# Sample attention of a decoder step: the third sequence's rope keys are turned earlier, and the last output but one is turned ahead of two score turnings

## The chip, the cores and the metric

The kernel runs on one core of a Trainium2 chip. The metric is the device time of one execution in microseconds (us); lower is better. Five engines work side by side: TensorE (PE, with its weight loads shown as PEld), VectorE (DVE), ScalarE (ACT), GpSimd (POOL) and SyncE (SP), which issues the loads of weights and cache pages. Each works through its own instructions in order, and they meet at semaphores.

## The reference, cut to what matters

The program is one inference step of a two-layer decoder. It serves one prompt of 512 tokens and 8 sample sequences of 8 new tokens, each with 2048 cached positions in 16 pages of 128. The change touches only the attention of the samples, which works on the latent cache:

```
past = cache_latent[l][page_table].reshape(8, 2048, 288)      # 256 latent | 32 rope
keys = concatenate([past, latent], axis=1)
q_lat = einsum('bqhn,chn->bqhc', q_nope, w_uk)
s = einsum('bqhd,bkd->bhqk', [q_lat | q_rope], keys) * ATTN_SCALE     # masked
p = softmax(s)
o_lat = einsum('bhqk,bkd->bqhd', p, keys[..., :256])
o = einsum('bqhc,chv->bqhv', o_lat, w_uv)
```

Ahead of it in a layer come the projections and the prompt's own attention, behind it the output projection, a convolved feed-forward part and, after both layers, a norm.

## The kernel before, in words

One program per engine is written out by hand, and the order in it is the order of execution. The order of TensorE in the sample attention, per layer, is `all_scores(0)`, then for b = 1 to 7 `all_scores(b)` and `all_values(b-1)`, then `all_values(7)` and `turn_output(7)`. So the values of a sequence come one place behind its scores, and between the scores of sequences 0 and 1 there are no values.

A sequence's 2048 keys lie in its pages with positions on the partitions. To be multiplied they are turned over (multiplied with the identity into PSUM, eight banks of 128 x 512) and copied to SBUF:

- `turn_rope(b)` (PE L1950) turns the 32 rope columns of all 16 pages into one bank (bank 6 for b > 0). It needs all 16 pages of the sequence: it waits for the four semaphores `pages_in[b % 3][g]`. DVE's `rope_keys(b)` (L1348) copies the bank to `ropeT[b % 2]`.
- `turn_keys(b, g)` (PE L1520, a helper's line that all turnings share) turns the latent part of four pages, for g = 0 to 3, into banks 4 and 5. ACT (`keys`, L805) and DVE (`keys`, L1352) copy one bank each.
- For b = 1 two more turnings follow `turn_keys(1, 0)`: those of the new tokens' latents `ckv`, into bank 7.
- `rope_scores(b)` (PE L1994) starts the scores in banks 0 to 3. For b > 0 it waits for `s_exp(b)`, the exponentials of sequence b-1 (ACT L820 and L822, released by a drain at L824), which read those banks. `scores(b, g)` (L2000) adds the latent part, and DVE takes the maxima (L1362 to L1387), which the exponentials wait for.
- `all_values(b)` turns the exponentials `sc` in five pieces (`turn_scores(b, g)`, L1520), copied to `pT` by ACT (g = 0 and 2, L829) and DVE (g = 1, 3 and 4, L1392 to L1400), and multiplies them with the pages (`values`, L2047, then L2076) into bank 7. DVE scales the result into `olat` (L1402), `turn_output(b)` turns it (L1520), and ACT copies it to `olatT` (`latent_output`, L811).

For the last sequence, `all_values(7)` holds `turn_output(6)`, behind `turn_scores(7, 0)`, `(7, 1)` and `(7, 2)`. The first values wait for `latent_output(6)`, since both use bank 7. ACT's order there is the copies of g = 0 and g = 2 and then `latent_output(6)`.

The pages have three buffers. SyncE issues one DMA of 144 KB per page, in order: the 16 pages of sequence 0, the 16 of sequence 1 (after the prompt's keys are assembled), and the 16 of sequence 2 (`keys_of(2)`, behind a wait for the last pair of prompt heads, `pv`). Then come the load of `wuv` (L491) and, from the third on, the pages of sequence b, each behind the values of sequence b-3 (`spv`, L478).

Of the kernel before, what the change touches and what calls it, by code (L numbers as in the profile page):

```python
# [31 lines left out]
TP, NB, NS = 512, 8, 8  # L32
# [51 lines left out]
def build(nc, A, O):  # L84
# [215 lines left out]
    kt_p, kt_d, kt_a = signal("kt_p", 5 * NB), signal("kt_d", 5 * NB), signal("kt_a", 4 * NB)  # L300
    newk_T, newk_ev = signal("newk_T", 1), signal("newk_ev", 1)
    s_p, s_new, new_ev = signal("s_p", 4 * NB), signal("s_new", NB), signal("new_ev", NB)
# [31 lines left out]
    def keys_bank(b, g):  # L334

        return 1 if b == 0 and g == 0 else 4

    def rope_bank(b):

# [8 lines left out]
    with nc.Block() as block:  # L348
# [208 lines left out]
        def _(act):  # L557
# [23 lines left out]
            for f in range(KD):  # L581
                act.wait_ge(start_T.sem, f + 1)
                b = 2 * (f % 2)
# [43 lines left out]
            for l in range(DEPTH):  # L627
# [173 lines left out]
                turned_probs(NH - 1)  # L801

                def keys(b, g):
                    act.wait_ge(kt_p.sem, kt_p.at(l, 5 * b + g + 2))
                    nc.scalar.activation(keysT[g % 2][:, 0, :], PS[:, keys_bank(b, g), :], ACT.Copy).then_inc(kt_a.sem, 1)  # L805

                def latent_output(b):

                    act.wait_ge(so_T.sem, so_T.at(l, b + 1))
                    for c in range(KC):  # L810
                        last = nc.scalar.activation(olatT[:, c, :, b, :], PS[:, 7, 256 + 128 * c:384 + 128 * c].rearrange("p (h s) -> p h s", h=NH), ACT.Copy)  # L811
                    last.then_inc(so_a.sem, 1)
# [10 lines left out]
                                         bias=softm[:, o + 6:o + 7], scale=SCALE, accum_out=softm[:, o + 8:o + 9])  # L823
                    nc.scalar.drain().then_inc(s_exp.sem, 1)  # L824

                def turned_scores(b):
                    for g in (0, 2):
                        act.wait_ge(spt_p.sem, spt_p.at(l, 5 * b + g + 1))
                        nc.scalar.activation(pT[:, 4 * g:4 * g + 4, :].rearrange("p a b -> p (a b)"), PS[:, 4 + g, :], ACT.Copy).then_inc(spt_a.sem, 1)  # L829

                for b in range(NB):
# [11 lines left out]
                    if b >= 1:  # L843
                        turned_scores(b - 1)
                    exponentials(b)
                turned_scores(NB - 1)
                latent_output(NB - 2)
                hi(l, U_OUT, 0, 0)
                hi(l, U_OUT + 1, 0, 1)

# [166 lines left out]
        def _(dve):  # L1017
# [105 lines left out]
            for l in range(DEPTH):  # L1123
# [220 lines left out]
                        last.then_inc(qrs_ready.sem, 1)  # L1344

                def rope_keys(b):
                    dve.wait_ge(kt_p.sem, kt_p.at(l, 5 * b + 1))
                    v.tensor_copy(ropeT[b % 2][:], PS[:, rope_bank(b), :]).then_inc(kt_d.sem, 1)  # L1348

                def keys(b, g):  # L1350
                    dve.wait_ge(kt_p.sem, kt_p.at(l, 5 * b + g + 2))
                    v.tensor_copy(keysT[g % 2][:, 1, :], PS[:, keys_bank(b, g) + 1, :]).then_inc(kt_d.sem, 1)  # L1352

                rope_keys(0)
# [15 lines left out]

                def scores(b):
                    o = 16 + 16 * (b % 2)
                    if b > 0:
                        rope_keys(b)
                        keys(b, 0)
                    keys(b, 1)
                    maximum(b, 0)
                    keys(b, 2)
                    maximum(b, 1)
                    keys(b, 3)  # L1380
                    maximum(b, 2)
                    new_scores(b)
                    maximum(b, 3)
                    v.drain()
                    v.tensor_reduce(softm[:, o + 5:o + 6], softm[:, o:o + 5], AX.X, ALU.max)
                    v.drain()
                    v.tensor_scalar(softm[:, o + 6:o + 7], softm[:, o + 5:o + 6], -SCALE, None, ALU.mult).then_inc(s_max.sem, 1)  # L1387
# [126 lines left out]
        def _(pe):  # L1514
# [170 lines left out]
            for l in range(DEPTH):  # L1685
# [152 lines left out]
                for i, (kind, m) in enumerate(GATE_UNITS):  # L1838
                    u = U_GATE + i
                    use(l, u)  # L1840
                    if kind == "pool":
                        if m == 0:
                            pe.wait_ge(last_ev.sem, last_ev.at(l, 1))
                        for t in range(4 * m, 4 * m + 4):
                            g = t // 2
# [93 lines left out]

                def turn_rope(b):  # L1940

                    if b >= 2:
                        pe.wait_ge(spt_a.sem, spt_a.at(l, 2 * (b - 1)))
                    if b >= 1:
                        pe.wait_ge(new_ev.sem, new_ev.at(l, b))
                    for g in range(4):
                        pe.wait_ge(pages_in[b % 3][g].sem, pages_in[b % 3][g].at(l, 16 * 4 * (b // 3 + 1)))
                    for t in range(4):
                        for g in range(4):
                            r = mm(PS[32 * g:32 * g + 32, rope_bank(b), 128 * t:128 * t + 128], pages[b % 3][:, 4 * g + t, KVL:LAT], ident[:], start=True, stop=True)  # L1950
                    r.then_inc(kt_p.sem, 1)

                def turn_keys(b, g):

                    if b >= 2 and g == 0:
                        pe.wait_ge(spt_a.sem, spt_a.at(l, 2 * (b - 1)))
                        pe.wait_ge(spt_d.sem, spt_d.at(l, 3 * (b - 1)))
                    if b > 0 or g > 0:
                        pe.wait_ge(kt_a.sem, kt_a.at(l, 4 * b + g))
                        pe.wait_ge(kt_d.sem, kt_d.at(l, 5 * b + g + (g > 0)))  # L1960
                    for c in range(KC):
                        for j in range(4):
                            r = turn(PS[:, keys_bank(b, g) + c, 128 * j:128 * j + 128], pages[b % 3][:, 4 * g + j, 128 * c:128 * c + 128], 128)
                    r.then_inc(kt_p.sem, 1)
# [19 lines left out]

                def rope_scores(b):

                    pe.wait_ge(kt_d.sem, kt_d.at(l, 5 * b + 1))
                    if b > 0:
                        pe.wait_ge(s_exp.sem, s_exp.at(l, b))
                    else:  # L1990
                        pe.wait_ge(kt_a.sem, kt_a.at(l, 1))
                        pe.wait_ge(kt_d.sem, kt_d.at(l, 2))
                    for g in range(4):
                        mm(PS[:, g, :], query(qrs[32 * g:32 * g + 32], b), ropeT[b % 2][32 * g:32 * g + 32, :], start=True, stop=False)  # L1994

                def scores(b, g):
                    pe.wait_ge(kt_a.sem, kt_a.at(l, 4 * b + g + 1))
                    pe.wait_ge(kt_d.sem, kt_d.at(l, 5 * b + g + 2))
                    for c in range(KC):
                        r = mm(PS[:, g, :], query(qlat[:, c], b), keysT[g % 2][:, c, :], start=False, stop=c == KC - 1)  # L2000
                    r.then_inc(s_p.sem, 1)
# [10 lines left out]
                    r.then_inc(so_T.sem, 1)  # L2012

                def all_scores(b):
                    if b > 0:
                        turn_rope(b)
                        turn_keys(b, 0)
                    if b == 1:
                        pe.wait_ge(o_done.sem, o_done.at(l, NH // 2))
                        for c in range(KC):  # L2020
                            r = turn(PS[0:TS, 7, 128 * c:128 * c + 128], ckv[:, c, TP:T], 128)
                        r.then_inc(newk_T.sem, 1)
                    rope_scores(b)
                    turn_keys(b, 1)
                    scores(b, 0)
                    if b >= 2:
                        turn_output(b - 2)
                    turn_keys(b, 2)
                    scores(b, 1)
                    turn_keys(b, 3)  # L2030
                    scores(b, 2)
                    new_scores(b)
                    scores(b, 3)
# [15 lines left out]
                def all_values(b):  # L2049
                    pe.wait_ge(s_exp.sem, s_exp.at(l, b + 1))  # L2050
                    if b + 1 < NB:
                        pe.wait_ge(new_ev.sem, new_ev.at(l, b + 2))
                    else:
                        pe.wait_ge(spt_a.sem, spt_a.at(l, 2 * b))
                        pe.wait_ge(spt_d.sem, spt_d.at(l, 3 * b))
                    turn_scores(b, 0)
                    turn_scores(b, 1)
                    turn_scores(b, 2)
                    if b == NB - 1:
                        turn_output(b - 1)  # L2060
                    if b == 0:
                        pe.wait_ge(newk_ev.sem, newk_ev.at(l, 1))
                    else:
                        pe.wait_ge(so_a.sem, so_a.at(l, b))
                    pe.wait_ge(spt_a.sem, spt_a.at(l, 2 * b + 1))
                    values(b, 0)
                    turn_scores(b, 3)
                    pe.wait_ge(spt_d.sem, spt_d.at(l, 3 * b + 1))
                    turn_scores(b, 4)
                    values(b, 1)  # L2070
                    pe.wait_ge(spt_a.sem, spt_a.at(l, 2 * b + 2))
                    values(b, 2)
                    pe.wait_ge(spt_d.sem, spt_d.at(l, 3 * b + 2))
                    values(b, 3)
                    pe.wait_ge(spt_d.sem, spt_d.at(l, 3 * b + 3))
                    mm(PS[:, 7, 0:KVL], pT[0:TS, NPG, :], newk[:], start=False, stop=True).then_inc(spv.sem, 1)  # L2076
# [150 lines left out]
```

## Time and profile before

| | us |
|---|---|
| Median of 3 runs | 2269.22 (2268.37 to 2270.55) |
| Profiled execution, its own time | 2268.8 |
| Its span, first to last instruction | 2267.0 |
| PE busy | 2217.9 (98%) |
| DVE / ACT / POOL busy | 1170.7 / 877.6 / 656.8 |
| Mean granted TensorE clock | 0.995 of full |

The span starts with the first instruction, and all times in the trace count from there. The profiled execution's own time is 1.8 us longer than its span. The first layer's sample attention runs from about 465 to 655 us, the second's from about 1577 to 1767 us. A busy share alone does not tell whether an engine sets the time; the wait of each instruction on PE does, and the rows below are of that kind.

### The profile page before, as it was taken

The numbers are of one execution on the slowest core, as the hardware profiler recorded it, in microseconds if no ns is written. First come the engines' busy times: TensorE is split into PE (matmuls) and PEld (weight loads), VectorE is DVE, ScalarE is ACT, GpSimd is POOL, SyncE is SP. The second block draws the span as 40 slices with busy tenths as digits, with TensorE's granted clock in tenths as the row PEclk, the third lists the DMA queues.
The fourth block names the chain that finished last, engine by engine and source line by source line (L and its number), as shares of the span: only waits on it lengthen the run. The fifth ranks groups of instructions, "written<-read, shape, count | busy, mean of one in ns | idle before, by whom it ended". The sixth has DMA issues, their size and how long they took to land.

```text
span 2267.0 us, 42639 instructions
## 1 busy us (share of the span) xinstructions
PE 2217.9 (98%) x16207; PEld 1988.3 (88%) x16207; DVE 1170.7 (52%) x1831; ACT 877.6 (39%) x1879; POOL 656.8 (29%) x316
## 2 busy tenths in 40 slices
PE   6999999999999999999999999999999999999998
PEld 5899997667789999999988999966677999999998
DVE  4443753844346666651153717457443476666433
ACT  4223225832233555541132332367222345555322
POOL 0223434400022333333322334332000323333332
PEclk9999999999999999999999999999999999999999
DMA  8554332033342222235545433212332422222322
GB/s 300 166 146 98 87 84 65 14 109 108 88 127 88 83 83 83 83 105 166 175 124 176 83 98 84 76 43 61 96 107 55 157 71 83 78 80 83 87 84 84
DMA packets 338278, 230.69 MB, mean 102 GB/s; under 512 B 62732, under 2 KB 321605, under 8 KB 338140
## 3 DMA queue, kind: packets, MB, share of 16 engines
q1 hardware_dynamic: 336594, 226.37, 34.8%
q10 hardware_dynamic: 1546, 2.43, 0.3%
q8 instruction: 92, 1.51, 0.3%
q14 instruction: 46, 0.38, 0.1%
HBM read 223.15 MB, written 5.60 MB: 101 GB/s over the span
## 4 chain that ended last, share of the span: by engine, by line
PE 93%; ACT 3%; DVE 2%; DMA 1%; issue 0%; DVEq 0%; SPq 0%; ACTq 0%
PE PS L1552 62%; PE PS L1520 6%; PE PS L2000 5%; PE PS L2047 5%; PE PS L1833 2%; PE PS L1596 2%; PE PS L1648 2%; PE PS L1936 2%; ACT prob L777 1%; PE PS L1569 1%; PE PS L1889 1%; PE PS L1912 1%; PE PS L1994 1%; PE PS L1950 1%; PE PS L2076 0%
## 5 line engine op out<-in xcount | busy, mean ns | idle before, releaser
L977 POOL TENSOR_TENSOR wlo<-raw,whi 128x1024 fp32r<-128x1024 f32 (+1 forms) x248 | 586.6, 2366 | 1503.0 <-ACT whi L563 1503.0
L563 ACT ACTIVATE whi<-raw 128x1024 fp32r<-128x1024 f32 (+1 forms) x252 | 258.6, 1026 | 927.1 <-PE PS L1552 852.2
L1552 PE MATMUL PS<-h_hi,whi 128*128 128x288 f32 x2496 | 538.6, 297 | 1.2 <-issue 1.0
L1552 PE MATMUL PS<-h_lo,whi 128*128 128x288 f32 x2496 | 535.4, 296 | 0.0
L1552 PE MATMUL PS<-h_hi,wlo 128*128 128x288 f32 x2496 | 535.0, 296 | 0.0
L1552 PEld LDWEIGHTS PS<-h_hi,whi 128*128 128x128 f32 x2496 | 402.4, 189 | 9.6 <-issue 8.8
L1552 PEld LDWEIGHTS PS<-h_lo,whi 128*128 128x128 f32 x2496 | 403.3, 188 | 0.0
L1552 PEld LDWEIGHTS PS<-h_hi,wlo 128*128 128x128 f32 x2496 | 403.2, 188 | 0.0
L1454 DVE TENSOR_SCALAR conv<-zext,convp 128x592 f32<-128x592 f32 x88 | 153.7, 1747 | 135.4 <-ACTq L896 135.0
L1552 PE MATMUL PS<-act_hi,whi 128*128 128x288 f32 x704 | 153.0, 299 | 0.0
L1552 PE MATMUL PS<-act_lo,whi 128*128 128x288 f32 x704 | 151.0, 296 | 0.0
L1552 PE MATMUL PS<-act_hi,wlo 128*128 128x288 f32 x704 | 150.9, 296 | 0.0
L2000 PE MATMUL PS<-keysT,qlat 128*128 128x512 f32 x256 | 122.1, 600 | 0.0
L2047 PE MATMUL PS<-pages,pT 128*128 128x256 f32 x512 | 117.0, 382 | 1.6 <-ACT olatT L811 1.6
L1552 PEld LDWEIGHTS PS<-act_hi,whi 128*128 128x128 f32 x704 | 113.2, 189 | 5.5 <-issue 5.3
L1552 PEld LDWEIGHTS PS<-act_lo,whi 128*128 128x128 f32 x704 | 113.8, 189 | 0.0
L1552 PEld LDWEIGHTS PS<-act_hi,wlo 128*128 128x128 f32 x704 | 113.6, 189 | 0.0
L2047 PEld LDWEIGHTS PS<-pages,pT 128*128 128x128 f32 x512 | 95.0, 190 | 15.0 <-ACT olatT L811 2.1
L1117 DVE SCALAR_TENSOR_TENSOR x<-PS,mod,x 128x288 f32<-128x288 f32 x32 | 16.6, 517 | 173.1 <-PE PS L1552 163.8
L805 ACT ACTIVATE keysT<-PS 128x512 f32<-128x512 f32 x64 | 38.3, 598 | 138.9 <-PE PS L1520 138.7
L1046 DVE TENSOR_TENSOR sumsq<-sumsq,tmp 128x576 f32<-128x576 f32 x30 | 49.1, 1637 | 80.3 <-ACT tmp L938 64.9
L1912 PE MATMUL PS<-k,q 96*128 96x128 f32 (+3 forms) x256 | 79.8, 454 | 6.1 <-ACT prob L777 6.1
(288 smaller groups left out, 3327.9 us busy)
## 6 DMA issues: line engine op xcount, KB each, us to landing
raw<-w_up SPq DMA_DIRECT2D x88, 512.0 KB, 3.8
pages<-cache_latent SPq DMA_DIRECT2D x256, 144.0 KB, 2.1
raw<-w_in SPq DMA_DIRECT2D x64, 512.0 KB, 4.0
ada_ring<-w_ada SPq DMA_DIRECT2D x41, 512.0 KB, 4.9
raw<-w_down SPq DMA_DIRECT2D x32, 512.0 KB, 3.9
ada_next<-w_ada SPq DMA_DIRECT2D x17, 512.0 KB, 4.1
ada_first<-w_ada SPq DMA_DIRECT2D x16, 512.0 KB, 10.4
raw<-w_out SPq DMA_DIRECT2D x16, 512.0 KB, 4.2
```

The costliest lines, as they stand in the source:

```text
L563: nc.scalar.activation(whi[:, slot, 0:width(u)], raw[:, slot, 0:width(u)], ACT.Copy).then_inc(hi_ready.sem, 1)
L977: nc.gpsimd.tensor_tensor(wlo[:, slot, 0:n], raw[:, slot, 0:n], whi[:, slot, 0:n].bitcast(F32), ALU.subtract).then_inc(lo_ready.sem, 1)
L1046: v.tensor_tensor(sumsq[:], sumsq[:], tmp[:, s, :], ALU.add).then_inc(sq_used.sem, 1)
L1454: v.tensor_scalar(c, zext[:, s, 2:ZE], convp[:, 1, bass.ds(f, 1)], convp[:, 1, bass.ds(f + 2 * KF, 1)], ALU.mult, ALU.add)
L1520: return nc.tensor.transpose(out, src, ident[0:k, 0:k])
L1552: r = mm(PS[0:m, 2 * (j % pairs) + half, 0:HT], w, o[:, k0 + k, half * HT:half * HT + HT], start=(first and k == 0 and part is whi and o i ...
L1596: r = mm(PS[:, 2 * s + half, 0:HT], part[:, s, 128 * k:128 * k + 128], o[:, k, half * HT:half * HT + HT], start=k == 0 and part is whi and ...
L1648: o = mm(PS[32 * j:32 * j + 32, 4 + r % 2, 0:256], cond[:, k, :], src[:, 256 * j:256 * j + 256], start=k == 0, stop=k == KD - 1)
L1833: r = mm(PS[:, bank, 0:c1 - c0], part[:, s, w0 + step * k:w0 + step * k + 128], o[:, k, c0:c1], start=(k == 0 and part is whi and o is xh) ...
L1912: mm(PS[:, qb, 0:128 * (qb + 1)], q96[:, s, 128 * qb:128 * qb + 128], k96[:, s, 0:128 * (qb + 1)], start=True, stop=True).then_inc(qk.sem, 1)
L2000: r = mm(PS[:, g, :], query(qlat[:, c], b), keysT[g % 2][:, c, :], start=False, stop=c == KC - 1)
L2047: mm(PS[:, 7, 0:KVL], pT[:, j, :], pages[b % 3][:, j, 0:KVL], start=j == 0, stop=False)
```

## The change

It has two parts, made in the programs of TensorE, VectorE and ScalarE; SyncE's and GpSimd's are as before. First, `turn_rope(2)` goes from the head of `all_scores(2)` into `all_scores(1)`, behind `turn_keys(1, 0)` and ahead of the two turnings of `ckv` and of `rope_scores(1)`. It waits for the copy of sequence 1's rope keys out of bank 6 and, as before, for all pages of sequence 2. DVE's `rope_keys(2)` goes to the matching place, between `keys(1, 0)` and `keys(1, 1)`, and the counts on the two semaphores are renumbered. Second, `turn_output(6)` comes right behind `turn_scores(7, 0)`, and ACT's `latent_output(6)` between the copies of g = 0 and g = 2.

```diff
+    def turned_rope(b):
+        return 8 if b == 2 else 5 * b + 1
+    def turned_keys(b, g):
+        return 5 * b + g + (3 if b == 1 and g > 0 else 2)
...                                                   ScalarE
-                turned_scores(NB - 1)
+                turned_scores(NB - 1, (0,))
                 latent_output(NB - 2)
+                turned_scores(NB - 1, (2,))
...                                                   VectorE, scores(b)
+                    if b == 1 or b > 2:
+                        rope_keys(b)
                     if b > 0:
-                        rope_keys(b)
                         keys(b, 0)
+                    if b == 1:
+                        rope_keys(2)
                     keys(b, 1)
...                                                   TensorE, turn_rope(b)
-                    if b >= 2:
+                    if b == 2:
+                        pe.wait_ge(kt_d.sem, kt_d.at(l, turned_rope(1)))
+                    elif b >= 1:
+                        pe.wait_ge(new_ev.sem, new_ev.at(l, b))
+                    if b > 2:
                         pe.wait_ge(spt_a.sem, spt_a.at(l, 2 * (b - 1)))
-                    if b >= 1:
-                        pe.wait_ge(new_ev.sem, new_ev.at(l, b))
                     for g in range(4):
                         pe.wait_ge(pages_in[b % 3][g].sem, pages_in[b % 3][g].at(l, 16 * 4 * (b // 3 + 1)))
...                                                   TensorE, all_scores(b)
+                    if b == 1 or b > 2:
+                        turn_rope(b)
                     if b > 0:
-                        turn_rope(b)
                         turn_keys(b, 0)
                     if b == 1:
+                        turn_rope(2)
                         pe.wait_ge(o_done.sem, o_done.at(l, NH // 2))
...                                                   TensorE, all_values(b)
                     turn_scores(b, 0)
+                    if b == NB - 1:
+                        turn_output(b - 1)
                     turn_scores(b, 1)
                     turn_scores(b, 2)
-                    if b == NB - 1:
-                        turn_output(b - 1)
```

## Rows read from the trace of the kernel before

**Rows 1.** The page: the span, and busy time (share of the span) xinstructions

```profile
span 2267.0 us, 42639 instructions
PE 2217.9 (98%) x16207; PEld 1988.3 (88%) x16207; DVE 1170.7 (52%) x1831; ACT 877.6 (39%) x1879; POOL 656.8 (29%) x316
```

**Rows 2.** Waits of PE, whole span: us in total, times, longest us

```profile
PE PS L1994 <- ACTq L824: 3.0, 2, 1.5
```

**Rows 3.** Timeline, sequence 1, layer 1: start, duration, engine, ... [idle before <-releaser]

```profile
476.97 1.08 PE L1950 MATMUL PS<-ident,pages 128*32 128x128 f32 x32
477.98 1.09 PE L1520 MATMUL PS<-ident,pages 128*128 128x128 f32 x8
...
478.74 0.68 DVE L1348 COPY ropeT<-PS 128x512 f32<-128x512 f32 x1
...
478.91 0.38 PE L1520 MATMUL PS<-ident,ckv 128*64 128x128 f32 x2
...
480.46 0.19 ACT L822 ACTIVATION_READ_ACCUMULATOR sc<-newsc,softm 128x1 f32 x1
...
480.81 1.14 PE L1994 MATMUL PS<-ropeT,qrs 32*128 32x512 f32 x8 [1.52 <-ACTq L824]
...
483.02 0.69 DVE L1352 COPY keysT<-PS 128x512 f32<-128x512 f32 x1 [3.00 <-PE PS L1520]
```

**Rows 4.** Timeline, SyncE: first and last page of sequence 2, layers 1 and 2

```profile
467.58 1.42 SPq L479 DMA_DIRECT2D pages<-cache_latent  x2
...
483.92 0.33 SPq L479 DMA_DIRECT2D pages<-cache_latent  x1
...
1595.31 0.33 SPq L479 DMA_DIRECT2D pages<-cache_latent  x1
```

**Rows 5.** Line L479, the issues at 483.92 and at 1595.31: us to landing

```profile
DMA to landing us min/median/max: 2.2/2.2/2.2
...
DMA to landing us min/median/max: 2.4/2.4/2.4
```

**Rows 6.** Timeline, layer 2, the rope scores of sequence 1

```profile
1592.56 1.14 PE L1994 MATMUL PS<-ropeT,qrs 32*128 32x512 f32 x8 [1.52 <-ACTq L824]
```

**Rows 7.** Timeline, layer 1, sequence 2: exponentials before it, first keys, rope scores

```profile
498.57 0.19 ACT L822 ACTIVATION_READ_ACCUMULATOR sc<-newsc,softm 128x1 f32 x1
...
503.02 1.09 PE L1520 MATMUL PS<-ident,pages 128*128 128x128 f32 x8
503.16 0.69 DVE L1348 COPY ropeT<-PS 128x512 f32<-128x512 f32 x1 [0.56 <-PE PS L1950]
...
504.05 1.14 PE L1994 MATMUL PS<-ropeT,qrs 32*128 32x512 f32 x8
```

**Rows 8.** Timeline, layer 1, the start of the last sequence's values

```profile
642.72 1.53 PE L1520 MATMUL PS<-ident,sc 128*128 128x128 f32 x12
...
642.83 0.48 DVE L1402 TENSOR_SCALAR olat<-PS,softm 128x256 f32<-128x256 f32 x1 [5.04 <-PE PS L2076]
...
644.28 0.60 ACT L829 ACTIVATE pT<-PS 128x512 f32<-128x512 f32 x1 [0.28 <-PE PS L1520]
...
644.77 0.44 ACT L811 ACTIVATE olatT<-PS 128x128 f32<-128x128 f32 x2
...
645.27 1.99 PE L2047 MATMUL PS<-pages,pT 128*128 128x256 f32 x8 [0.80 <-ACT olatT L811]
```

**Rows 9.** Timeline, PE, the first matmul after its longest wait past 20 us

```profile
45.43 0.58 PE L1596 MATMUL PS<-h_hi,whi 128*128 128x288 f32 x1 [4.07 <-DVE h_lo L1089]
```

**Rows 10.** Windows: length, busy (x) of PE, PEld, DVE, ACT, POOL, PEclk, DMA, GB/s

```profile
43.00:44.00 1.00, 0.00 (x0) 0.00 (x0) 0.93 (x3) 0.71 (x1) 0.00 (x0) 0.95 1.08 285
...
50.00:51.00 1.00, 1.00 (x7) 1.00 (x6) 1.00 (x2) 0.61 (x1) 0.00 (x0) 0.64 1.04 396
...
46.00:50.00 4.00, 4.00 (x19) 4.00 (x18) 4.00 (x7) 2.27 (x4) 0.00 (x0) 0.50 1.01 342
...
52.00:56.00 4.00, 4.00 (x33) 4.00 (x32) 3.22 (x5) 1.45 (x2) 0.00 (x0) 1.00 0.12 49
```

More of the change, by code:

```diff
@@ L803, in keys @@
                 def keys(b, g):
-                    act.wait_ge(kt_p.sem, kt_p.at(l, 5 * b + g + 2))
+                    act.wait_ge(kt_p.sem, kt_p.at(l, turned_keys(b, g)))
                     nc.scalar.activation(keysT[g % 2][:, 0, :], PS[:, keys_bank(b, g), :], ACT.Copy).then_inc(kt_a.sem, 1)
@@ L824, in exponentials, with turned_scores @@
                     nc.scalar.drain().then_inc(s_exp.sem, 1)
-                def turned_scores(b):
-                    for g in (0, 2):
+                def turned_scores(b, groups=(0, 2)):
+                    for g in groups:
                         act.wait_ge(spt_p.sem, spt_p.at(l, 5 * b + g + 1))
@@ L1346, in rope_keys @@
                 def rope_keys(b):
-                    dve.wait_ge(kt_p.sem, kt_p.at(l, 5 * b + 1))
+                    dve.wait_ge(kt_p.sem, kt_p.at(l, turned_rope(b)))
                     v.tensor_copy(ropeT[b % 2][:], PS[:, rope_bank(b), :]).then_inc(kt_d.sem, 1)
                 def keys(b, g):
-                    dve.wait_ge(kt_p.sem, kt_p.at(l, 5 * b + g + 2))
+                    dve.wait_ge(kt_p.sem, kt_p.at(l, turned_keys(b, g)))
                     v.tensor_copy(keysT[g % 2][:, 1, :], PS[:, keys_bank(b, g) + 1, :]).then_inc(kt_d.sem, 1)
@@ L1959, in turn_keys @@
                         pe.wait_ge(kt_a.sem, kt_a.at(l, 4 * b + g))
-                        pe.wait_ge(kt_d.sem, kt_d.at(l, 5 * b + g + (g > 0)))
+                        pe.wait_ge(kt_d.sem, kt_d.at(l, turned_keys(b, g - 1) if g > 0 else turned_keys(b - 1, 3)))
                     for c in range(KC):
@@ L1985, in rope_scores @@
                 def rope_scores(b):
-                    pe.wait_ge(kt_d.sem, kt_d.at(l, 5 * b + 1))
+                    pe.wait_ge(kt_d.sem, kt_d.at(l, turned_rope(b)))
                     if b > 0:
@@ L1997, in scores @@
                     pe.wait_ge(kt_a.sem, kt_a.at(l, 4 * b + g + 1))
-                    pe.wait_ge(kt_d.sem, kt_d.at(l, 5 * b + g + 2))
+                    pe.wait_ge(kt_d.sem, kt_d.at(l, turned_keys(b, g)))
                     for c in range(KC):
```

## The prediction

> **What bounds the kernel now.** I read the page first: PE is busy for 98% of the span [rows 1], so the time is PE's own work plus its few waits, and a change counts by what it does to PE's order of work. Then the list of PE's waits: the wait ahead of `rope_scores(1)` for the exponentials of sequence 0 stands there with 3.0 us, 1.5 us in each of the two layers [rows 2]. The timeline around it shows what PE, DVE and ACT do there [rows 3]. Last I read the queue that nobody shows among PE's waits, SyncE's page loads [rows 4], since the moved turning reads pages.
>
> **Part 1, the wait that is to be filled.** PE starts the two `ckv` turnings at 478.91; they end at 478.91 + 0.38 = 479.29, and `rope_scores(1)` starts at 480.81, behind the last exponential (480.46 + 0.19 = 480.65) [rows 3]. The turning itself takes 477.98 - 476.97 = 1.01 us of PE, start to next start [rows 3]. By the engines alone it would fit: bank 6 is copied out at 478.74 + 0.68 = 479.42, so `turn_rope(2)` could start at 479.5, end its issue at 480.5, and with 0.3 us for the `ckv` turnings (from their 0.38, less the overlap of the last one's end) `rope_scores(1)` would start at 480.8, where it starts today. DVE's added copy (0.69 us) lies in the 3.00 us that DVE idles ahead of 483.02 [rows 3]; without that cover it would delay `keys(1, 1)` by the same 0.69.
>
> **Part 1, the pages.** The moved turning keeps its wait for all 16 pages of sequence 2. SyncE issues them one by one: the first at 467.58, the last at 483.92, which is (483.92 - 467.58) / 15 = 1.09 us apart [rows 4], and no part of the change makes this earlier. They follow the pages of sequence 1 without a gap, so it is SyncE's pace and not the `pv` wait that places them. The last page lands 2.2 us after its issue [rows 5], at 486.12. Before, `turn_rope(2)` came at about 502 us and never saw this. Now PE stands at it from 477.98 + 1.09 = 479.07 to about 486.2 (0.1 us for the release, my choice; a semaphore from DVE or ACT took about that). PE works in order, and queued behind are the `ckv` turnings, `rope_scores(1)` and everything after, on which ACT and DVE wait in turn. `rope_scores(1)` then starts at 486.2 + 1.01 + 0.3 = 487.5, which is 6.7 us late. In the second layer the last page is issued at 1595.31 [rows 4] and takes 2.4 us [rows 5]: 1597.7, PE goes on at 1597.8, `rope_scores(1)` at 1599.1 against 1592.56 [rows 6], 6.55 us late. Together **+13.25 us**. Bounds: the landing may move by 0.3 us in each layer, so 12.6 to 13.9. Nothing behind takes it back: the later page loads and those of `w_out` wait for the values on PE, and shift with them.
>
> **Part 1, what is saved for sequence 2.** The turning's 1.01 us goes from the head of `all_scores(2)`. There too, `rope_scores(2)` follows the start of `turn_keys(2, 0)` by 504.05 - 503.02 = 1.03 us, because DVE's rope copy ends only at 503.16 + 0.69 = 503.85 [rows 7]; the same eight turnings take 478.91 - 477.98 = 0.93 us where the next work is free [rows 3]. With the copy done long ago 0.10 us more goes, 1.11 us per layer. What is late next is `s_exp(2)`, and it is ready at 498.57 + 0.19 = 498.76 [rows 7], four microseconds ahead of the new start. The copies of `turn_keys(2, 0)` would end some 0.7 us after it, 0.2 us ahead of when PE asks for the banks, about even. **-2.2 us** for two layers; bounds 1.9 to 2.3.
>
> **Part 2, the last output but one.** PE waits 0.80 us for ACT's `olatT` copies ahead of `values(7, 0)` at 645.27 [rows 8]; the other layer has its like. New order: `turn_scores(7, 0)` is a third of the twelve turnings that take some 1.3 us, issued by 643.15; `turn_output(6)` needs `olat`, which ends at 642.83 + 0.48 = 643.31 [rows 8], so a new wait of 0.2 us stands there, with the eight other turnings queued behind it. Its result is in PSUM at about 643.8. ACT has copied g = 0 by 644.0 and then does the two `olatT` copies (0.44 us [rows 8]), to 644.45. PE's turnings end their issue at 644.3 + 0.2 = 644.5, so `values(7, 0)` starts at about 644.55 instead of 645.27, 0.7 us sooner. The copy of g = 2 (0.60 us) ends at about 645.35 instead of 644.88, needed only for `values(7, 2)` two microseconds later. **-1.4 us** for both layers. Bounds: 0, if PE's new wait eats it, to 1.6, the whole wait.
>
> **The clock.** Nowhere in PE's work after the first 20 us does it idle for 7 us; the nearest row is 4.07 us, ended at 45.43 [rows 9]. There the granted clock falls from full (2.4 GHz) to half (1.2 GHz): 0.95 in the window from 43 to 44 puts the fall at 43.9, and 0.64 from 50 to 51 puts the rise at 50.7 [rows 10]. So PE worked at half clock from 45.43 to 50.7, 5.3 us. Four such microseconds hold 19 matmuls, four at full clock 33; less two of each that overlap the edges, 17 against 31, so 45% of the time is lost [rows 10]: 5.3 x 0.45 = 2.4 us. I take the same for each layer, since a 7.1 us idle is longer than that: **+4.8 us**. Bounds: 0, if the clock does not fall, and 3.1 a layer (45% of the whole 6.8 us of half clock in that place), 6.2 in all.
>
> The Trainium skill, in "TensorE: Matmul & The Clock Gate", section "Terms", prices a throttled stretch as its whole duration times the share of the clock that is missing. The idle part counts in that. Here the clock would be low from about 2.5 us into the idle (481.6) to 491.5, 9.9 us, so 4.95 us a layer by that rule instead of my 2.4, and 9.65 + 9.9 = 19.55 us in all instead of 14.45. In the row above the rule would give 3.4 us where 2.4 are lost, for the first 1.5 us of half clock had no work in them; I go by the row.
>
> **The sum.** 13.25 - 2.2 - 1.4 + 4.8 = +14.45 us, on the profiled execution's 2268.8 (span 2267.0, 1.8 around it): 2283.25. From the median of the runs shown, 0.4 above it, it would be 2283.7. I forecast **2283.4**.
>
> **The rivals.**
> - The pages wait is there, but the clock stays up or its fall costs nothing. For it: the wait at 4.07 us is the only row of its kind, in another kind of work. Against: this idle is longer. 13.25 - 2.2 - 1.4 = +9.65, so 2278.6.
> - The clock costs as the rule counts it, or the half clock lasts longer than in the row: +19.55, 2288.4. Against it is that no work lies in the idle.
> - The other side: the turning fits into its wait. This decides on the last page's landing. At 479.5 or before, nothing is late, and the kernel gains 2.2 + 1.4 = 3.6 us, 2265.4; the gain per layer is 1.8, so a landing at 481.3 would be even. In its favour is that all engine times fit to 0.1 us. Against it are the issue and landing times, 4.8 us past that point in layer 1, and an unchanged SyncE. Only if the timed runs' loads ran well ahead of the profiled one's could it be; their times differ by 0.4 us, so I see none of that.
> - The change does not do what it says, the wait being passed or shifted elsewhere so that the two ends cancel: within 0.2%.
>
> **How the numbers follow.** My forecast (pages and half clock as in the row) 0.78, no clock cost 0.13, more clock cost 0.04, the other side 0.03, no change 0.02. The forecast's own range with the bounds of its terms is 2280.5 to 2286. To leave out no more than 2 in 10 and take in the case without clock cost and its error, the range goes from 2277 to 2286.5. A measurement of this kernel can tell 0.2% (4.5 us) from no change: all three slower cases lie over that, so slower has 0.95, faster (all of 3.6 us, 0.16%, counts half as same) 0.02, same 0.03.
>
> **What would show it.** In the changed kernel PE would have a wait of about 7 us ahead of L1950, released by the DMA of pages, twice, in place of the 1.5 us for L824; the granted clock would be 0.5 for some 9 us from the middle of that wait, and its mean about 0.991 instead of 0.995. `rope_scores(2)` would follow `turn_keys(2, 0)` by 0.93. The wait ahead of L2047 for `olatT` would be gone or below 0.2 us. The prediction is wrong if L1950 of sequence 2 starts at 479.5, if the last page lands before 481, or if PE runs at full clock behind the idle.

## The result, and the profile after

| | us, median (range) | runs | ratio to before |
|---|---|---|---|
| Before | 2268.37 (2266.77 to 2270.55) | 5 | |
| After | 2280.02 (2277.98 to 2283.16) | 5 | 1.0054 [1.0043, 1.0065] |

The ratio stands with its 95% interval. The change makes the kernel 11.65 us slower by the medians; the forecast time was 2283.4 us, 3.4 us above the median after. The profiled execution of the changed kernel took 2277.98 us (span 2276.2) and is the fastest of its five, which matters below. Of the 11 runs of `part2_alone` below, one took 3108.17 us at a mean granted clock of 0.655 and is left out of its ratio. The changed kernel's line numbers are higher: L1950 is now L1964, L1994 is L2008, L2047 is L2063.

The list of PE's waits, whole span (us in total, times, longest us), answers to [rows 2]. The wait for the exponentials (there L1994) and the wait for `olatT` (L2047) are gone, and a wait for pages leads the list:

```profile
PE PS L1964 <- DMA pages<-cache_latent: 13.3, 2, 6.7
PE PS L1532 <- DMA rows_in<-x_sample: 7.2, 1, 7.2
```

The timeline around sequence 1 in layer 1 answers to [rows 3]:

```profile
475.61 1.08 PE L1964 MATMUL PS<-ident,pages 128*32 128x128 f32 x32
476.62 1.09 PE L1532 MATMUL PS<-ident,pages 128*128 128x128 f32 x8
477.39 0.69 DVE L1357 COPY ropeT<-PS 128x512 f32<-128x512 f32 x1
...
479.10 0.19 ACT L830 ACTIVATION_READ_ACCUMULATOR sc<-newsc,softm 128x1 f32 x1
...
482.48 0.43 SPq L499 DMA_DIRECT2D wuv<-w_uv  x1
484.33 1.94 PE L1964 MATMUL PS<-ident,pages 128*32 128x128 f32 x32 [6.61 <-DMA pages<-cache_latent]
486.19 0.64 PE L1532 MATMUL PS<-ident,ckv 128*64 128x128 f32 x2
486.76 1.68 PE L2008 MATMUL PS<-ropeT,qrs 32*128 32x512 f32 x8
488.38 1.10 PE L1532 MATMUL PS<-ident,pages 128*128 128x128 f32 x8
```

Bank 6 is free at 478.08 and the exponentials are done at 479.29. PE stands until 484.33, some two microseconds behind SyncE's last page issue, which comes right ahead of the `wuv` load at 482.48. Then everything takes longer: the turning 1.86 us to the next start instead of 1.01, the rope scores 1.62 instead of 1.07. The windows of single microseconds, with the columns of [rows 10] (PEclk is the third number from the end), tell why:

```profile
480.00:481.00 1.00, 0.00 (x0) 0.00 (x0) 0.00 (x0) 0.00 (x1) 0.00 (x0) 1.00 0.45 127
481.00:482.00 1.00, 0.00 (x0) 0.00 (x0) 0.00 (x0) 0.00 (x0) 0.00 (x0) 0.54 0.52 138
...
486.00:487.00 1.00, 1.00 (x13) 0.43 (x10) 0.68 (x1) 0.13 (x1) 0.00 (x0) 0.50 0.82 336
487.00:488.00 1.00, 1.00 (x8) 0.28 (x8) 0.01 (x1) 0.24 (x1) 0.00 (x0) 0.54 0.00 0
488.00:489.00 1.00, 1.00 (x10) 0.63 (x7) 0.00 (x0) 0.00 (x0) 0.00 (x0) 1.00 0.00 0
```

The granted clock falls to half (1.2 GHz) at 481.1, 3.4 us into the idle, and is full again at 487.9. In layer 2 the same windows put the fall at 1597.2, 3.2 us into the idle, and the rise at 1604.9. The head of sequence 2 and the start of the last values answer to [rows 7] and [rows 8]:

```profile
508.51 1.09 PE L1532 MATMUL PS<-ident,pages 128*128 128x128 f32 x8
...
509.53 1.14 PE L2008 MATMUL PS<-ropeT,qrs 32*128 32x512 f32 x8
...
648.20 0.66 PE L1532 MATMUL PS<-ident,sc 128*128 128x128 f32 x4
648.31 0.48 DVE L1414 TENSOR_SCALAR olat<-PS,softm 128x256 f32<-128x256 f32 x1 [5.04 <-PE PS L2092]
648.85 0.44 PE L1532 MATMUL PS<-ident,olat 128*128 128x128 f32 x2
...
649.12 1.04 PE L1532 MATMUL PS<-ident,sc 128*128 128x128 f32 x8
649.39 0.44 ACT L819 ACTIVATE olatT<-PS 128x128 f32<-128x128 f32 x2
650.00 1.89 PE L2063 MATMUL PS<-pages,pT 128*128 128x256 f32 x8
```

**Where the time went.** Each place is read by how much later PE is than in the trace before. `turn_rope(1)` starts 475.61 - 476.97 = -1.36, `turn_keys(1, 1)` 488.38 - 481.88 = +6.50: +7.86 in this place. The head of sequence 2 is at 508.51 - 503.02 = +5.49: -1.01. The first values of sequence 7 are at 650.00 - 645.27 = +4.73, from +5.48 at the turnings ahead of them: -0.75, and 0.10 more goes in the 8 matmuls there. Layer 2 gives the same: +7.85, -1.00, -0.75, -0.10. The sum is 15.71 - 2.01 - 1.70 = **+12.0 us**, near the medians' 11.65. The two profiled spans differ by only 9.2, since 2.8 us come from stretches that the change does not touch: 1.36 ahead of the first layer's sample attention, and 1.45 between the two, in the prompt's attention of layer 2. These rows (before, then after) give the prompt scores' shortest, median and longest ns, and first and last start: from first to last 72.8 us before and 71.2 after, and single matmuls of up to 1058 ns before.

```profile
L1912 PE MATMUL PS<-k,q x128: 272/486/1058, 1493.4 to 1566.2; 96*128 96x128 f32 x32, 96*128 96x256 f32 x32, 96*128 96x384 f32 x32, 96*128 96x512 f32 x32
```
```profile
L1924 PE MATMUL PS<-k,q x128: 273/484/697, 1498.1 to 1569.3; 96*128 96x128 f32 x32, 96*128 96x256 f32 x32, 96*128 96x384 f32 x32, 96*128 96x512 f32 x32
```

### The profile page after: what moved, and what is told of

Read it like the earlier page. It is cut to its first block, busy times and chain, and to the rows that moved or that the text cites. A ratio compares the mean times of both kernels' runs of the same rounds, so it can differ in the third digit from the quotient of the medians.

```text
span 2276.2 us, 42637 instructions
## 1 busy us (share of the span) xinstructions
PE 2216.8 (97%) x16207; PEld 1985.0 (87%) x16207; DVE 1169.3 (51%) x1831; ACT 877.3 (39%) x1879; POOL 656.3 (29%) x316
## 4 chain that ended last, share of the span: by engine, by line
PE 85%; issue 5%; SPq 4%; POOLq 3%; DVE 1%; DMA 1%; ACT 0%; POOL 0%; DVEq 0%; ACTq 0%
PE PS L1564 62%; PE PS L2063 5%; PE PS L1532 5%; PE PS L2014 4%; POOLq L992 2%; PE PS L1608 2%; PE PS L1845 2%; PE PS L1660 1%; SPq L486 1%; PE PS L1581 1%; SPq L487 1%; SPq L385 1%; POOLq L1010 1%; PE PS L2008 1%; PE PS L1964 1%
## 5 line engine op out<-in xcount | busy, mean ns | idle before, releaser
L2063 PE MATMUL PS<-pages,pT 128*128 128x256 f32 x512 | 116.8, 381 | 0.0
L2063 PEld LDWEIGHTS PS<-pages,pT 128*128 128x128 f32 x512 | 94.8, 190 | 13.1
L1468 DVE SCALAR_TENSOR_TENSOR conv<-zext,convp,conv 128x592 f32<-128x592 f32 x88 | 77.8, 884 | 14.7 <-issue 14.1
```

Of the source, the lines that this page charges most:

```text
L1468: v.scalar_tensor_tensor(c, zext[:, s, 1:ZE - 1], convp[:, 0, bass.ds(f + 2 * KF, 1)], c, ALU.mult, ALU.add)
L2063: mm(PS[:, 7, 0:KVL], pT[:, j, :], pages[b % 3][:, j, 0:KVL], start=j == 0, stop=False)
```

## The experiments

All were timed against the kernel before, each in five or more runs. Its median was 2267.8 to 2268.2 in them.

**1. The pages early, the change kept (`early_after`), and the same without the change (`early_before`).** SyncE looks the page numbers up ahead of the waits; both kernels have the same edit:

```diff
+                found = look_up(1)
                 sp.wait_ge(k_asm.sem, k_asm.at(l, NH))
-                keys_of(1)
+                keys_of(1, found)
+                found = look_up(2)
                 sp.wait_ge(pv.sem, pv.at(l, NH // 2))
-                keys_of(2)
+                keys_of(2, found)
```

> The changed kernel, but SyncE looks the page numbers of sequences 1 and 2 up in the table ahead of the waits for the prompt's attention, so that only the DMA issue is left per page (0.33 us of the 1.09). My theory, the landing of the pages sets the cost: the last page of sequence 2 lands near 473 to 475 us, before PE reaches the moved turning at about 479.5, so PE's wait of 6.6 and 6.7 us goes, and the clock's fall with it. The time is below the kernel before by 2 x 1.0 (turning in the old wait) + 1.7 (last output) = 3.7 us: about 2264.7. Rival, the turning's new place itself costs (a bank, a copy, PE's order): the time stays near 2280.

Measured: 2264.0 us, ratio 0.9982 [0.9973, 0.9991]. The wait is gone; in `early_after`'s timeline PE goes from one turning to the next with only the wait for the rope copy:

```profile
478.15 1.08 PE L1969 MATMUL PS<-ident,pages 128*32 128x128 f32 x32
479.16 1.09 PE L1537 MATMUL PS<-ident,pages 128*128 128x128 f32 x8
...
480.66 1.08 PE L1969 MATMUL PS<-ident,pages 128*32 128x128 f32 x32 [0.41 <-DVE ropeT L1362]
...
482.01 1.14 PE L2013 MATMUL PS<-ropeT,qrs 32*128 32x512 f32 x8
```

The rope scores start 482.01 - 478.15 = 3.86 us behind `turn_rope(1)`, against 3.84 in [rows 3]. The turning fits into the wait at no cost.

> The kernel before with the same earlier look-up. My theory: nothing on PE waits for these pages there, so the time stays within 0.5 us of the kernel before, 2268.4. Rival, that earlier page loads help or hurt by themselves (through the queue or through SBUF traffic beside the prompt's attention): a change of 2 us or more, which would have to be taken off the reading of the other kernel.

Measured: 2267.97 us, ratio 1.0002 [0.9993, 1.0011], and the two waits for the exponentials are there as before. So the earlier pages are worth nothing by themselves (the interval leaves room for 0.1%), and 16 us of the changed kernel's 2280.0 hang on when they land.

**2. Each part alone.** `part1_alone` undoes this in the changed kernel, and `part2_alone` is the kernel before with this (and the parameter that ScalarE's helper needs for it) and nothing else:

```diff
-                turned_scores(NB - 1)
+                turned_scores(NB - 1, (0,))
                 latent_output(NB - 2)
+                turned_scores(NB - 1, (2,))
...
                     turn_scores(b, 0)
+                    if b == NB - 1:
+                        turn_output(b - 1)
                     turn_scores(b, 1)
                     turn_scores(b, 2)
-                    if b == NB - 1:
-                        turn_output(b - 1)
```

> The changed kernel without its second part (the last output is turned where it was before). My theory: the second part is worth 1.7 us and independent of the first, so this comes to 2280.0 + 1.7 = 2281.7, with two waits of 6.6 us for the pages. Rival, the parts share a wait: as the changed kernel, 2280.0.

Measured: 2282.21 us, ratio 1.0059 [1.0045, 1.0073], pages waits of 6.5 and 7.2 us.

> The kernel before with only the last output turned earlier. My theory: 0.85 us per layer goes (0.75 of the wait for the olatT copies, 0.10 behind it), 1.7 us in all: about 2266.7. Rival, the gain is given back at the next wait of that stage (the output projection waits for the h_lo copies): 2268.4.

Measured: 2265.66 us, ratio 0.9991 [0.9982, 1.0000]. The gain is 2.1 us by the medians, at the edge of what can be told; its trace has the wait ahead of the values gone and the same order and spacing as the changed kernel's. The parts add up: part 1 alone costs 2282.2 - 2268.2 = 14.0 us, and 14.0 - 2.1 = 11.9 is near the 11.65 of both.

**3. The wait without the move (`wait_alone`),** on the kernel before:

```diff
                     if b == 1:
+                        for g in range(4):
+                            pe.wait_ge(pages_in[2][g].sem, pages_in[2][g].at(l, 16 * 4))
                         pe.wait_ge(o_done.sem, o_done.at(l, NH // 2))
```

> The kernel before with only a wait added on PE: ahead of the ckv turnings of sequence 1 it waits for all pages of sequence 2; the turning stays at the head of all_scores(2), nothing else is changed. My theory, the wait alone makes the loss: ckv and the rope scores of sequence 1 start some 5 us late per layer, at 1.5 us of half clock: 2268.0 + 2 x (5.1 + 1.4) = about 2281. Rival, the moved work (its bank, its copy, the renumbered counts) makes part of it: clearly below that, down to 2268.

Measured: 2283.81 us, ratio 1.0068 [1.0055, 1.0082], with waits of 6.7 and 7.3 us for the pages. That is more than the 2281 expected, and its trace shows a term that was sized too small: the expectation took 1.5 us of clock cost per layer, and here it is 3.1 and 2.5 us (reckoned as in the table below). PE worked at half clock for 6.5 and 5.3 us behind the wait, against 3.6 and 4.2 in the changed kernel. This kernel lacks part 2, so its fair neighbour is `part1_alone`, 2282.21, and the 1.6 us between them are within the spread of either. A wait on semaphores, with no work moved, makes the whole loss of part 1.

**4. The idle filled (`filled`),** to keep the clock up:

```diff
                     if b == 2:
                         pe.wait_ge(kt_d.sem, kt_d.at(l, turned_rope(1)))
+                        for i in range(44):
+                            turn(PS[:, 6, 128 * (i % 4):128 * (i % 4) + 128], ident[:], 128)
```

> The changed kernel with 44 turnings of the identity into the free bank 6 ahead of the moved turning's wait for the pages: 44 x 0.108 = 4.7 us of work in an idle of 6.6 us; the results are written over and used by nobody. My theory, the clock's fall costs 1.6 us per layer: PE keeps its full clock, the pages wait shrinks to about 1.5 us, PE goes on at the same moment (the landing sets it), and the time is 3.2 us below the changed kernel: about 2276.8. Rival, the half clock hides beside other waits: 2280.0, unchanged.

Measured: 2278.78 us, ratio 1.0045 [1.0031, 1.0059]. The clock stayed full and the turning took 1.01 us again:

```profile
479.60 5.02 PE L1532 MATMUL PS<-ident 128*128 128x128 f32 x44 [0.41 <-DVE ropeT L1357]
...
485.95 1.08 PE L1966 MATMUL PS<-ident,pages 128*32 128x128 f32 x32 [1.32 <-DMA pages<-cache_latent]
486.96 0.41 PE L1532 MATMUL PS<-ident,ckv 128*64 128x128 f32 x2
487.30 1.14 PE L2010 MATMUL PS<-ropeT,qrs 32*128 32x512 f32 x8
```

The total alone does not settle the clock's cost: 1.2 us below the changed kernel is less than the spread of either. The stage does. Its end is the start of the new scores of sequence 1, the matmuls with the sequence's own new keys (L2005 in the kernel before, L2019 in the changed one). From the moment PE goes on to that point, this kernel takes 10.25 us in both layers; the changed one takes 11.88 and 11.75. The expected gain of 3.2 us is thus in the stage (3.1), and the last page held PE 0.65 us longer in this execution than in the changed kernel's.

**5. The landing in doses.** All four kernels are `early_after` with fewer look-ups ahead, and the edits are shown against it. The first two doses were badly designed:

```diff
-                found = look_up(1)
+                found = look_up(1, 4)        # 8 in eight_early
...
-                found = look_up(2)
                 sp.wait_ge(pv.sem, pv.at(l, NH // 2))
-                keys_of(2, found)
+                keys_of(2)
```

> The changed kernel with only 4 page numbers of sequence 1 looked up ahead, each 0.57 us (page pace 1.09 with, 0.52 without the look-up): the last page of sequence 2 lands 2.3 us sooner, PE's idle is 4.3 us per layer instead of 6.6. The clock fell 3.6 to 3.8 us into the idle in the changed kernel. Theory: 2280.0 - 4.6 = 2275.4 if the clock still falls and stays low as long, and 2272.3 if it doesn't fall. Rival, the page wait is not what carries the time: 2280.

Measured: 2280.96 us, ratio 1.0056 [1.0042, 1.0069].

> The same with 8 looked up ahead: the last page lands 4.6 us sooner, PE's idle is 2.0 us per layer and the clock stays up. Theory: 2280.0 - 9.2 - 3.1 = 2267.7, near the kernel before (the break-even that the prediction put at a landing 1.8 us behind the one that costs nothing). Rival, the clock's fall costs nothing: 2270.8.

Measured: 2277.21 us, ratio 1.0040 [1.0026, 1.0054]. Neither theory held, and `four_early` came out near its rival's 2280. This does not speak for the rival, since the edits hardly moved the landing: 5.9 and 6.2 us of PE's wait are left in the one, 5.7 and 6.2 in the other. SyncE reached sequence 2 sooner, and then stood at the `pv` wait, for the last product of the prompt's attention. Its own waits in the kernel with eight early, 380 to 520 us, show it:

```profile
SPq L489 <- PE PS L1952: 3.9, 1, 3.9
```

Behind it the 16 pages kept their 1.09 us each. (The fall of the clock 3.6 to 3.8 us into the idle, which the expectation names, is 3.4 and 3.2 us by the windows.) The doses that do act put the look-ups into sequence 2 (6 and 3 of 16, beside all of sequence 1):

```diff
-                found = look_up(2)
+                found = look_up(2, 6)        # 3 in second_3
```

> A mended dose. In the two kernels with 4 and 8 look-ups of sequence 1 ahead, the pages of sequence 2 still could not start before the pv wait (their buffer is in use), only 2 to 4 us sooner than SyncE came anyway, and kept their own pace of 1.09 us. Here all 16 of sequence 1 and 6 of sequence 2 are looked up ahead: from the pv wait (about 10.5 us ahead of turn_rope(1)... counted from its start, at -10.5) the 16 issues take 6 x 0.52 + 10 x 1.09 = 14.0 us and the last lands 2.2 us later, at +5.2, where the kernel with all looked up goes on at +2.5. My theory: 2264.0 + 2 x 2.7 = 2269.4, idle of PE some 4 us; more by 1.5 to 3 us per layer if the clock falls in it (2272.4 to 2275.4). Rival, only the landing of all pages long before matters: near 2280.

Measured: 2270.37 us, ratio 1.0014 [1.0005, 1.0023]. That lies between the theory's two cases, 2269.4 with the clock up and 2272.4 with it down, and the total does not tell them apart. The trace does: the clock fell in both layers, and PE went on at +4.4 and +4.8 us instead of +5.2.

> The same with 3 of sequence 2 looked up ahead: the last page lands 3 x 0.57 = 1.7 us later still, at +6.9. My theory: 2264.0 + 2 x 4.4 + 2 x (1.5 to 3.1, the clock falls in an idle of 5.7 us) = 2275.8 to 2279.0. Rival without a clock cost: 2272.8.

Measured: 2276.83 us, ratio 1.0034 [1.0021, 1.0048], inside the 2275.8 to 2279.0 of the theory and off the rival's 2272.8.

**What the doses show together.** In the profile of each kernel, counted from the start of `turn_rope(1)` in layers 1 and 2: when PE goes on with the moved turning, and when it reaches the new scores of sequence 1 (the stage). The clock's cost is the stage less the first number less 10.25.

| kernel | PE goes on at | stage, us | clock's cost |
|---|---|---|---|
| before | | 12.75, 12.75 | |
| early_after | 2.51, 2.51 | 12.77, 12.77 | 0 |
| second_6 | 4.40, 4.82 | 16.18, 16.58 | 1.5, 1.5 |
| second_3 | 6.33, 6.61 | 19.26, 19.10 | 2.7, 2.2 |
| eight_early | 7.82, 8.31 | 20.99, 21.49 | 2.9, 2.9 |
| four_early | 8.03, 8.29 | 21.04, 20.20 | 2.8, 1.7 |
| part1_alone | 8.65, 9.33 | 21.77, 22.07 | 2.9, 2.5 |
| after | 8.72, 8.85 | 20.60, 20.60 | 1.6, 1.5 |
| filled | 8.86, 9.36 | 19.11, 19.61 | 0 |

2264.0 plus what both stages exceed 12.77 gives 2271.2 for `second_6` (measured 2270.37), 2276.8 for `second_3` (2276.83) and 2279.7 for the changed kernel (2280.02). The other four fit less well: 2279.7 for `four_early` (2280.96), 2280.9 for `eight_early` (2277.21), 2277.2 for `filled` (2278.78) and, with 1.7 added for the missing part 2, 2284.0 for `part1_alone` (2282.21). The stage is that of one execution and the time is a median; the profiled execution of `eight_early` was the slowest of its five, 2282.03. So the three close agreements are partly chance, and totals are told to some 2 to 4 us. Within the stage the account is closer: at full clock it lasts 10.25 us from the moment PE goes on, whether that comes at 2.51 or at 9.36 us, so the lateness of the pages is passed on one to one, and the clock adds 1.5 to 2.9 us a layer on top.

## Why the prediction was right

**The pages wait (+13.25 forecast).** Right in mechanism: the named semaphore holds PE, in both layers, for 6.6 and 6.7 us, and taking the late landing away (experiment 1) takes the whole loss away. PE went on at 8.72 and 8.85 us behind the start of `turn_rope(1)`, where the forecast had 9.23 (486.2 - 476.97) and 9.08. At full clock the rope scores would follow by 1.35 us, as in experiment 1, so they are late by 10.07 - 3.84 = 6.23 and 10.20 - 3.84 = 6.36, 12.6 us in all. The forecast's 0.7 too much has two parts. In layer 1 PE went on 0.5 us sooner because the 32 page issues took 34.67 us here and 35.15 in the trace before. In layer 2 they took the same (34.77 and 34.74), and the 0.2 lies in the landing, for which 2.4 us and 0.1 for the release were taken.

**The clock (+4.8).** Right that it falls, and the size is right on average: 2.4 us a layer were forecast, and the twelve falls in the table cost 2.2 on average. The profile after is at the cheap end with 1.6 and 1.5, so the term was sized too large for it by 1.7 us in the two layers. Half clock behind the idle lasted 3.6 us in its layer 1, and 4.2 in layer 2, against the 5.3 that [rows 10] gave. Of the signs that were named, the low clock lasted 6.8 and 7.7 us where some 9 were forecast, and the mean was 0.994 in this execution (0.991 to 0.994 in the five) where 0.991 was. The Trainium skill's price in "TensorE: Matmul & The Clock Gate", section "Terms" (the throttled duration times the missing share), gives an estimate of 6.8 x 0.5 = 3.4 us for layer 1, half clock from 481.1 to 487.9, where 1.6 were lost. This trace does not agree with it, as in [rows 10]: of the 6.8 us, 3.2 had no work in them.

**Saved for sequence 2 (-2.2).** -2.0 measured. The turning's 1.01 us went as said, but the 0.10 for the missing rope copy did not: `rope_scores(2)` still follows `turn_keys(2, 0)` by 509.53 - 508.51 = 1.02 us, where 0.93 were forecast. The 0.93 was read ahead of two other turnings, so it was no price for what precedes rope scores. Nobody waits for the copy there any more, and the time stays; what it is spent on no run shows.

**The last output (-1.4).** -1.7 measured: 0.75 for the wait, as worked out (0.7), and 0.10 behind it, which the step did not have, so the term came out just above its own upper bound of 1.6. The small new wait for `olat` is there: the turning starts at 648.85, against 648.63 if it had followed its four predecessors at 0.1 us each.

**The other rivals.** "No clock cost" is excluded by the clock's rows and by the stage in experiment 4; by the total alone (2278.6 for it, 2280.02 measured) it could not be told from the forecast. "The other side" has its mechanism right too: `early_after` gains 3.8 us where the rival had 3.6 for pages that land in time. What ruled it out was only SyncE's pace. The even point of 1.8 us of lateness was not met by any dose: `second_6`, 1.9 and 2.3 us late, is 2.5 us slower than before; the clock fell in it at 1.5 us a layer, which that rival's arithmetic left out.

The sum of the terms in the profile is 12.6 + 3.1 - 2.0 - 1.7 = +12.0 against +14.45 forecast; of the 2.45 between them 1.7 is the clock's and 0.7 the landing's, and the other two terms are off by +0.2 and -0.3. Part of the agreement with the medians is luck: with the mean fall of 2.2 us a layer the sum would be +13.3, and the medians' +11.65 lies 1.7 us below that. No run settles whether the falls were cheap in the executions that were not profiled.

Two readings of the forecast's range have to be put right. Its "own range", 2280.5 to 2286, is not the sum of its terms' bounds: they give 12.6 - 2.3 - 1.6 = +8.7 at the least and 13.9 - 1.9 + 6.2 = +18.2 at the most, 2277.5 to 2287.0 on the profiled 2268.8. The measured 2280.02 lies below that own range, and inside the stated one of 2277 to 2286.5, which was widened for the case without a clock cost.

## What to carry to other kernels

Before work is moved into a wait, look at what the work reads, not only at which engine is idle: a load that had sixteen microseconds of slack in the old place made PE wait nearly seven in the new one, and the list of waits of the kernel before cannot show it. Follow the issuing queue to its last transfer of that data. Where the queue is slow because it looks addresses up, doing this ahead of a wait it has anyway turned a loss of 11.7 us into a gain of 3.8.

## What the runs showed of the hardware

Two things were not expected. First, the clock fell behind a short wait too: in `second_6`, layer 1, PE waited 2.3 us behind turnings, and the clock fell at about 483.4, when PE had been at work again for 0.9 us; it came back at 486.8. In layer 2 PE waited 2.7 us, and the clock was at half from 1596.1, the end of the wait, to 1599.5. The columns are those of [rows 10]:

```profile
482.47 1.12 PE L1969 MATMUL PS<-ident,pages 128*32 128x128 f32 x32 [2.29 <-DMA pages<-cache_latent]
```
```profile
482.00:483.00 1.00, 0.53 (x20) 0.56 (x24) 0.00 (x0) 0.46 (x1) 0.00 (x0) 1.00 0.67 209
483.00:484.00 1.00, 1.00 (x23) 0.46 (x14) 0.37 (x1) 0.00 (x0) 0.00 (x0) 0.69 1.02 422
...
486.00:487.00 1.00, 1.00 (x9) 0.90 (x6) 0.00 (x0) 0.00 (x0) 0.00 (x0) 0.60 0.00 0
```

The 1.5 us wait of the kernel before, and in `filled` two short ones with 5 us of matmuls between them (0.4 and 1.3 us, in layer 2 0.4 and 1.8), did not bring it down. Second, two thirds of a page's 1.09 us on SyncE are not the DMA's issue. In the trace before, the look-up's own instructions (ns min/median/max) stand beside it; with them out of the way (`early_after`) a page took 0.52 to 0.54 us.

```profile
L478 SPq TENSOR_LOAD <-tab x256: 262/268/471, 379.2 to 1724.5; - x128
L478 SPq FUSED_REGOPS  x256: 152/152/174, 379.7 to 1724.8; - x128
...
L479 SPq DMA_DIRECT2D pages<-cache_latent x256: 332/333/988, 380.2 to 1725.2; - x128
```
